# Differential attention scores from the second head on: one float32 product, or three float32r products of split q and k

## The reference

```python
def diff_attention(h, w_in, q_norm, k_norm, lq1, lk1, lq2, lk2, sub_norm, lambda_init):
    proj = (h @ w_in).astype(f32)
    q, k, v = jnp.split(proj, 3, axis=-1)
    q = rms_norm(q.reshape(bsz, L, DIFF_HEADS, 2, DIFF_DK), q_norm) * (DIFF_DK ** -0.5)
    k = rms_norm(k.reshape(bsz, L, DIFF_HEADS, 2, DIFF_DK), k_norm)
...
        bias = -slopes * jnp.abs(qpos[:, None] - kpos[None, :])
        s = jnp.einsum('bqhzd,bkhzd->bzhqk', qblk, k) + bias[None, None]
        p = jax.nn.softmax(s, axis=-1)
        attn = p[:, 0] - lam * p[:, 1]
        return jnp.einsum('bhqk,bkhe->bqhe', attn, v)
...
    o = rms_norm(o, sub_norm) * (1.0 - lambda_init)
```

## Time and profile before

| | |
|---|---|
| median of 3 runs | 2486.63 us (2485.77 to 2487.23) |
| the profiled execution, its own time | 2487.29 us |
| its span, first to last instruction | 2485.5 us |
| granted TensorE clock, mean | 0.996 |
| PE busy | 2432.7 us, 98% |
| DVE busy | 1514.8 us, 61% |
| ACT busy | 1141.8 us, 46% |
| scores of S | items start between 1171 and 1277 us |
| scores of P | items start between 1688 and 1862 us |

### The profile page before, as it was taken

One profiled execution on the slowest core, in us unless ns is written; L12 is line 12 of the kernel. 1 busy time (PEld: TensorE's weight loads), 2 busy tenths in 40 slices (PEclk: granted clock), 3 DMA queues, 4 the chain that ended last, 5 costly groups with the idle time before them and its releaser, 6 DMA issues.

```text
span 2485.5 us, 35278 instructions
## 1 busy us (share of the span) xinstructions
PE 2432.7 (98%) x14135; PEld 2065.6 (83%) x14135; DVE 1514.8 (61%) x2568; ACT 1141.8 (46%) x2002; POOL 0.2 (0%) x4
## 2 busy tenths in 40 slices
PE   9999899999999999999999999999999999999999
PEld 5887776778898999898788888778788898888887
DVE  8899558776566755564655446657895554533332
ACT  4323446364444655644454434536764443523432
POOL 0000000000000000000000000000000000000000
PEclk9999999999999999999999999999999999999999
DMA  5435542264223565344224323223334423433322
GB/s 194 103 75 136 201 127 73 84 205 173 86 76 102 179 186 170 119 128 127 77 76 159 107 92 119 76 85 102 94 94 137 135 77 94 141 95 95 101 93 93
DMA packets 110722, 291.34 MB, mean 117 GB/s; under 512 B 18944, under 2 KB 41600, under 8 KB 109280
## 3 DMA queue, kind: packets, MB, share of 16 engines
q1 hardware_dynamic: 99088, 260.38, 33.9%
q10 hardware_dynamic: 11472, 28.71, 3.5%
HBM read 267.45 MB, written 19.50 MB: 115 GB/s over the span
## 4 chain that ended last, share of the span: by engine, by line
PE 76%; DVE 8%; ACT 3%; issue 1%; DMA 1%; SPq 0%; ACTq 0%; DVEq 0%
PE ps L1439 66%; PE ps L1505 2%; PE ps L1530 2%; PE ps L1548 1%; DVE wlo L1416 1%; PE ps L1572 1%; DVE ps L1723 1%; DVE ps L1722 1%; DVE yP L1724 1%; ACT yP L1591 1%; DMA wraw<-wt 1%; PE ps L1471 1%; PE ps L1954 1%; PE ps L1561 0%; ACT yP L1592 0%
## 5 line engine op out<-in xcount | busy, mean ns | idle before, releaser
L1411 ACT ACTIVATE whi<-wraw 128x1024 fp32r<-128x1024 f32 x430 | 452.0, 1052 | 195.4 <-PE ps L1439 129.3
L1439 PE MATMUL ps<-in_hP,whi 128*128 128x512 f32 x1336 | 540.0, 404 | 1.6 <-issue 1.6
L1416 DVE TENSOR_TENSOR wlo<-wraw,whi 128x1024 fp32r<-128x1024 f32 x430 | 522.1, 1218 | 4.7 <-ACT whi L1411 4.4
L1439 PE MATMUL ps<-in_hP,wlo 128*128 128x512 f32 x1336 | 522.0, 391 | 0.0
L1439 PE MATMUL ps<-in_lP,whi 128*128 128x512 f32 x1336 | 521.0, 390 | 0.0
L1439 PE MATMUL ps<-in_hS,whi 128*128 128x256 f32 x1088 | 319.5, 294 | 5.6 <-DVE x L1745 4.3
L1439 PE MATMUL ps<-in_lS,whi 128*128 128x256 f32 x1088 | 309.0, 284 | 0.0
L1439 PE MATMUL ps<-in_hS,wlo 128*128 128x256 f32 x1088 | 308.9, 284 | 0.0
L1439 PEld LDWEIGHTS ps<-in_hP,whi 128*128 128x128 f32 x1336 | 251.5, 188 | 62.9 <-issue 11.3
L1439 PEld LDWEIGHTS ps<-in_lP,whi 128*128 128x128 f32 x1336 | 251.6, 188 | 55.5 <-issue 5.0
L1439 PEld LDWEIGHTS ps<-in_hP,wlo 128*128 128x128 f32 x1336 | 251.2, 188 | 53.9
(11 more groups left out here) (475 smaller groups left out, 3627.4 us busy)
## 6 DMA issues: line engine op xcount, KB each, us to landing
wraw<-wt SPq DMA_DIRECT2D x432, 512.0 KB, 3.5
wraw<-wt ACTq DMA_DIRECT2D x17, 512.0 KB, 4.2
k_scratch<-region_P SPq DMA_DIRECT2D x16, 256.0 KB, 3.1
v_scratch<-vtmp SPq DMA_DIRECT2D x32, 128.0 KB, 3.2
x<-x_in SPq DMA_DIRECT2D x4, 768.0 KB, 7.1
mix_mem<-mem_in ACTq DMA_DIRECT2D x1, 2048.0 KB, 10.5
x<-x_in ACTq DMA_DIRECT2D x1, 2048.0 KB, 12.8
region_S<-k_scratch ACTq DMA_DIRECT2D x2, 1024.0 KB, 5.8
```

The lines of the kernel that those rows point to most:

```text
L1411: nc.scalar.activation(whi[:, (n + 3) % NHI, :, :], wraw[:, ws(n), :, :], ACT.Copy).then_inc(wh.sem, 1)
L1416: nc.vector.tensor_tensor(wlo[:, ws(n), :, :], wraw[:, ws(n), :, :], whi[:, (n + 3) % NHI, :, :].bitcast(F32), ALU.subtract).then_inc(wr.s ...
L1439: last = nc.tensor.matmul(ps[:, m % 2, 0:N[prod.g]], w_[:, k, :], x_[:, k, :], start=(k == 0 and j == 0), stop=(k == KT - 1 and j == 2))
```

## The change

For the first head of each group nothing changes. From head 1 on the scores are the sum of three float32r products: high q by high k, low q by high k, high q by low k. The parts of head h+1 are made during the second item (b = 1) of head h: ACT writes the high parts of q and k into `in_h[g][:, h+1]` and `in_l[g][:, h+1]`, whose output of that head comes later, and DVE writes the low parts over q and k themselves. PE waits for the low parts (`att_lo`) at the first item of each head. In the S group the second item of head h is the last one before head h+1; in the P group two more items follow.

```diff
+                def to_split(self, t):
+                    h, b = self.item(t)
+                    return h + 1 if b == 1 and h + 1 < DH else None
...
-                    for zz in range(2):
-                        rows = slice(64 * zz, 64 * zz + 64)
-                        last = nc.tensor.matmul(ps[:, 3 + zz, 0:N[g]], dq[g][rows, h, b * P:(b + 1) * P], dk[g][rows, h, :],
-                                                start=True, stop=True)
+                    js = slice(b * P, (b + 1) * P)
+                    if h == 0:
+                        parts = ((dq[g][:, 0, js], dk[g][:, 0, :]),)
+                    else:
+                        parts = ((in_h[g][:, h, js], in_l[g][:, h, :]), (hid_h[g][:, h, js], in_l[g][:, h, :]),
+                                 (in_h[g][:, h, js], hid_l[g][:, h, :]))
+                        if b == 0:
+                            pe.wait_ge(att_lo.sem, a.lo + h)
+                    for i, (q_part, k_part) in enumerate(parts):
+                        for zz in range(2):
+                            rows = slice(64 * zz, 64 * zz + 64)
+                            last = nc.tensor.matmul(ps[:, 3 + zz, 0:N[g]], q_part[rows], k_part[rows],
+                                                    start=(i == 0), stop=(i == len(parts) - 1))
                     last.then_inc(sc_done.sem, 1)
...
+            def act_diff_high(a, d_, qkv_, t):
+                g, h = d_.g, d_.to_split(t)
+                if h is None:
+                    return
+                if h == 1:
+                    a.wait_ge(td.sem, qkv_.last + 1)
+                    a.wait_ge(gs[g]["ap"].sem, qkv_.ap + 16)
+                nc.scalar.activation(in_h[g][:, h, :], dq[g][:, h, :], ACT.Copy)
+                nc.scalar.activation(in_l[g][:, h, :], dk[g][:, h, :], ACT.Copy).then_inc(att_hi.sem, 1)
...
+            def dve_diff_low(v, d_, t):
+                g, h = d_.g, d_.to_split(t)
+                if h is None:
+                    return
+                v.wait_ge(att_hi.sem, d_.hi + h)
+                nc.vector.tensor_tensor(hid_h[g][:, h, :], dq[g][:, h, :], in_h[g][:, h, :].bitcast(F32), ALU.subtract)
+                nc.vector.tensor_tensor(hid_l[g][:, h, :], dk[g][:, h, :], in_l[g][:, h, :].bitcast(F32), ALU.subtract)\
+                    .then_inc(att_lo.sem, 1)
...
                             elif step[0] == "diff":
                                 act_diff_copy(a, step[1], step[3])
+                                act_diff_high(a, *step[1:])
...
                             elif step[0] == "diff":
                                 dve_diff_out(v, step[1], step[3])
+                                dve_diff_low(v, step[1], step[3])
```

More of the change, by code:

```diff
@@ L1007, in trunk_tail @@
                 "sc", "neg", "exp", "prob", "tr", "trc", "out", "ofree"))
+            att_hi, att_lo = sig("att_hi"), sig("att_lo")
             lam_a, disl = sig("lam_a"), sig("disl")
@@ L1082, in __init__ @@
                     self.ob = ofree.base
+                    self.hi, self.lo = att_hi.take(DH - 1), att_lo.take(DH - 1)
                     self.sq = z["sqd"].take(DH)
```

## The result

| | before | after |
|---|---|---|
| median | 2486.68 us (4 runs) | 2515.3 us (4 runs, 2513.38 to 2517.24) |
| ratio | | 1.0118, 95% interval 1.0106 to 1.013 |
| span of the profiled execution | 2485.5 | 2511.6 |

A forecast was written before the change was run, and what follows sets the result against it. S was taken as bound by PE alone, P by PE with DVE close behind. 19.5 - 0.7 - 0.5 + 4.5 = +22.8 on 2487.3 gives 2510.1, the median 0.7 lower: 2509.5 us, range 2502 to 2519.

The forecast's parts named there:

- the clock: S stage: granted clock falls behind none to seven new PE gaps, 0 to 10.3 us; three taken, +4.5 us.
- DVE in P: P stage: two subtractions, 1.22 us a head, absorb most of PE's gain; P in all -0.5 us, between -3 and +3.
- The wait at each new head of S: S stage: PE idles for the split before each new head's scores, seven waits, 19.5 us in all.
- PE's products in S: S scores: three float32r products take 0.58 us instead of 0.63, 0.05 gained for each of 14 items, 0.7 us.
- PE's products in P: P scores: three float32r products take 0.92 us, 0.14 gained for each of 28 items, 3.9 us if PE were alone.
- The halves: Rival, S and P scores: the two halves of a float32r product do not run together; about 2528 us, chance 0.07.
- the hidden loads: Rival, S and P scores: second and third parts' loads are not hidden, 0.2 us an item; 2515 us, chance 0.08.
- The faster case: Rival: the split is ready before the scores, leaving only PE's gain; 2482 to 2485 us, chance 0.03.
- a shorter wait without a loss of clock: Rival, S stage: waits of only 1.5 us a head and no clock loss; 2498 us, chance 0.05.

The follow-up runs named there:

- s_early: The kernel after, with the parts of each S head made one slot earlier, in the previous head's first item: 2485.57 us, ratio 0.9998.
- s_fill: The kernel after, with 10 to 13 unread matmuls on PE ahead of the wait at each new S head: 2505.34 us, ratio 1.0078.
- s_only: The kernel after, with P scores left as one float32 product without a split, S still split: 2514.87 us, ratio 1.0116.
- p_no_low: s_early without low parts in P: no DVE subtraction, second and third product repeat the first, so scores differ in value: 2482.36 us, ratio 0.9985.
- p_apart: s_early, with P's high parts on ACT in the second item's slot and low parts on DVE in the third's: 2482.56 us, ratio 0.9984.
- p_pool: s_early, with P's low parts made by GpSimd instead of DVE: 2485.84 us, ratio 1.0.
- p_third: s_early, with P's parts made in the slot of a head's third item instead of its second: 2490.45 us, ratio 1.0019.

## Why the prediction was right, and where its terms were off

The predicted 2509.5 us and range of 2502 to 2519 hold the measured 2515.3, and the mechanism that makes up nearly all of the loss is the predicted one. Two terms were sized wrongly, the clock and DVE in P, both to the low side, and P's came out with the other sign.

- **The wait at each new head of S.** Forecast 2.5 us four times, 3.3, 2.9 and 3.3, in all 19.5. Measured 2.51 four times, 3.41, 3.01, 3.40: 19.9. s_early takes it away, s_fill leaves it standing alone at 19.8 us.
- **The clock, the term that was mis-sized.** I took three stretches of 1.5 us, 4.5. There were five lengths of 1.6 or a little less, counting the long one twice, in the profiled execution, 7.7 us, and 9.2 us in the median by s_fill; the upper bound that I had worked out was 10.3. By the medians this term is 4.7 of the 5.8 us by which the forecast was short. Its price for one was right. Its number was a guess, and that it stayed inside the range is in part luck: I had shown two gaps, of 3.4 us with a fall and of 1.9 without, and set the new ones between them. The trace of before has others. One of 2.25 us (ending 246.91) and one of 1.51 us (ending 617.94) are followed by the lower level, one of 2.12 us (ending 118.10) is not:

```profile
247.10:250.50 3.40, 3.40 (x17) 3.40 (x17) 3.26 (x6) 0.62 (x2) 0.00 (x0) 0.50 0.61 242
```

  So the length of the gap does not by itself put the cases in order, and no row told how many of seven would fall. The number also differs between executions with the same gaps: five lengths in the trace of after, six in that of s_only.
- **PE's products in S.** 0.05 us an item forecast, 0.08 measured (1.07 for 14): 0.7 against 1.07 us.
- **PE's products in P.** 0.14 us an item forecast, 0.15 to 0.16 measured: a slot of 5.45 is now 5.29 or 5.30. The forecast took its fixed part and a float32 pass from the clock (0.213 us); no row shows a single float32 pass, only the block.
- **DVE in P.** Forecast -0.5 us, measured +0.7, within its bounds. A head of 22.9 us was forecast, 0.2 under before, and takes 23.0, 0.07 under. The fourth item's scores do wait for DVE, by 0.17 to 0.21 us. The first head cost 1.7 us where I took 1.3. p_no_low shows that it is DVE, p_apart that it is only DVE's place. The wait at the second item's `neg` was in the forecast's chain (scores of the third item at 10.13); it was in my expectations for p_pool and p_no_low, a head of 22.5 us, that I left it out.
- **The halves and the hidden loads.** Both rivals fell. The one of the loads that are not hidden did not fall by the time, since it had given 2515 us, which is what was measured. It is the rows that rule it out: the block is 0.89 us in P and 0.55 in S from its first start to the next product, under the 0.92 and 0.58 of the forecast, where that rival needs 0.2 more. In the trace of after the loads of the second and third part (PEld) start while the part before runs (PE):

```profile
1779.07 0.19 PEld L1563 LDWEIGHTS ps<-in_lP,in_hP 64*128 64x128 f32 x2 [0.76 <-issue]
1779.18 0.19 PEld L1563 LDWEIGHTS ps<-in_lP,hid_hP 64*128 64x128 f32 x2
1779.41 0.19 PEld L1563 LDWEIGHTS ps<-hid_lP,in_hP 64*128 64x128 f32 x2
```
```profile
1779.07 0.50 PE L1563 MATMUL ps<-in_lP,in_hP 64*128 64x512 f32 x2
1779.40 0.39 PE L1563 MATMUL ps<-in_lP,hid_hP 64*128 64x512 f32 x2
```

- **The faster case** named its condition, parts made before the tile ends. s_early meets it for S; P's place had to be changed as well before the kernel beat the one before.
- **A sum that does not come out.** The rival of a shorter wait without a loss of clock is put at 2498 us for 1.5 us a head. Seven waits of 1.5 us and the other terms give 2486.6 + 10.5 - 0.7 - 0.5 = 2496. Nothing else hangs on it.

## What to carry to other kernels

Preparing an operand cost nothing that could be measured here where every engine has idle time, but only at the right place in each list: ask not how idle an engine is but what its list releases last before the new work, and who waits behind it. Where engines that work in order hand a value on within one slot, look at what the second then stands for; here it helped to put the two steps into different slots. And where PE is made to stand, add the clock to the price: here 8 to 9 us on top of 20 for seven gaps of 2.5 to 3.4 us. Shorter gaps were not safe from it: one of 1.67 us in p_third was followed by the lower level too. Which gaps are, no run here shows.

## What the runs showed of the hardware that was not expected

- The same gap may or may not be followed by the lower clock: a gap of 3.40 us (after, ending 1295.17) was followed by none, one of 2.51 us (ending 1239.34) had 6.8 us of it, from 1238.93 on, one of 1.67 us in p_third (ending 1740.34) had 3.4 us, and s_only, with gaps equal to 0.01 us, had a different set.
- Matmuls of rows 0 to 63 and of rows 64 to 127 run as two streams. Placed three and three in the list instead of by turns, they still start in pairs, and the block stays 0.89 us from its first start to the next product.
- GpSimd's work is not free for DVE: beside it, DVE's instructions with two SBUF inputs took 1.82 instead of 0.75 us and 1.99 instead of 1.22. Instructions with one tensor input were held up in some places too: a TENSOR_SCALAR of 128x512 took 1.28 instead of 0.49 us (p_pool, 1719.36), and the small one that writes `neg` 1.16 instead of 0.17 (1790.39).
- In the block of three float32r products, 512 wide, the second and third matmul of a half start 0.23 us apart, and the first and second 0.33 (after, 1767.38, 1767.72, 1767.95). The whole block takes 0.89 or 0.90 us where the float32 one took 1.06, so that the change gained 0.16 us an item.
